# Grouped-query attention and the modulated norms of a chained transformer kernel: the values' projection moved last, the last queries' head work moved beside it and into the pair loop, rounding one step later, norms in fused pieces

## The reference, cut to what matters

```python
h = rms_norm(x, g_norm[i]) * (1.0 + sc) + sh        # twice in each layer; sc, sh differ for tokens and context

z = h @ w_qkv                                       # 1024 -> 16 query heads, 4 key heads, 4 value heads of 64
q, k = rms_norm(q, g_q), rms_norm(k, g_k)           # over the 64 features of each head
q, k = apply_rope(q, cos, sin), apply_rope(k, ...)  # only for the 256 tokens, not for the context
p = softmax(q @ k.T * 64**-0.5)                     # tokens see 512 keys, context sees 256
y = merge(p @ v) @ w_out
x = x + gate * y
```

## Time and profile before

| | us |
|---|---|
| median of 3 executions | 3028.16 (3027.71 to 3032.05) |
| the profiled execution | 3027.03 |
| its span, first to last instruction | 3025.2 |
| PE busy in the span | 2884.8 (95%) |
| DVE busy | 1829.3 (60%) |
| ACT busy | 1187.3 (39%) |
| POOL busy | 305.2 (10%) |

### The profile page before, as it was taken

The page is one execution under the profiler, slowest core; times in us unless marked ns, Lnnn a source line. Parts: engine busy times, 40 slices in busy tenths (PEclk is TensorE's granted clock), DMA queues, the critical chain, the costliest instruction groups (busy, mean ns, idle before and its releaser), DMA issues.

```text
span 3025.2 us, 43358 instructions
## 1 busy us (share of the span) xinstructions
PE 2884.8 (95%) x18438; PEld 2347.4 (78%) x18438; DVE 1829.3 (60%) x2548; ACT 1187.3 (39%) x1667; POOL 305.2 (10%) x284
## 2 busy tenths in 40 slices
PE   8999888998999999999999999998999999998999
PEld 7888888997864788877657887875678887774899
DVE  4477766555456466664875677556646775546454
ACT  3245564445234422234244222344442223425443
POOL 1000001101000201112011111200120011000110
PEclk9999999999999999999999999999999999998999
DMA  8836324454211244432113444330034443211353
GB/s 294 332 132 238 126 84 168 170 189 159 98 42 42 91 188 153 183 138 99 69 43 139 153 181 167 125 109 29 16 139 165 171 179 112 99 70 42 140 181 126
DMA packets 59617, 407.01 MB, mean 135 GB/s; under 512 B 6520, under 2 KB 9848, under 8 KB 11168
## 3 DMA queue, kind: packets, MB, share of 16 engines
q1 hardware_dynamic: 58224, 400.00, 36.1%
q0 software_dynamic: 1200, 4.23, 0.5%
HBM read 402.60 MB, written 1.09 MB: 133 GB/s over the span
## 4 chain that ended last, share of the span: by engine, by line
PE 83%; DVE 8%; ACT 5%; issue 2%; POOL 0%; DMA 0%; DVEq 0%; ACTq 0%
PE bank L600 25%; PE bank L602 24%; PE bank L601 24%; DVE wlo L1970 3%; ACT whi L1336 2%; PE bank L1089 1%; ACT part L1593 1%; PE bank L1139 1%; PE bank L1214 1%; PE bank L1083 1%; PE bank L700 1%; PE bank L1093 1%; ACT xnhi L1596 1%; PE bank L1230 1%; PE bank L724 0%
## 5 line engine op out<-in xcount | busy, mean ns | idle before, releaser
L1970 DVE TENSOR_TENSOR wlo<-raw,whi 128x2048 fp32r<-128x2048 f32 x281 | 647.3, 2304 | 457.4 <-ACT whi L1336 457.3
L1336 ACT CAST whi<-raw 128x2048 fp32r<-128x2048 f32 x281 | 535.3, 1905 | 617.8 <-PE bank L602 612.1
L600 PE MATMUL bank<-xnhi,whi 128*128 128x512 f32 (+1 forms) x1760 | 663.6, 377 | 39.2 <-DVE xnlo L2383 18.8
L602 PE MATMUL bank<-xnhi,wlo 128*128 128x512 f32 (+1 forms) x1760 | 649.6, 369 | 0.0
L601 PE MATMUL bank<-xnlo,whi 128*128 128x512 f32 (+1 forms) x1760 | 647.8, 368 | 0.0
L600 PEld LDWEIGHTS bank<-xnhi,whi 128*128 128x128 f32 x1760 | 336.0, 191 | 136.7 <-issue 59.9
L602 PEld LDWEIGHTS bank<-xnhi,wlo 128*128 128x128 f32 x1760 | 336.1, 191 | 57.0
L601 PEld LDWEIGHTS bank<-xnlo,whi 128*128 128x128 f32 x1760 | 336.6, 191 | 53.8 <-issue 0.2
L600 PE MATMUL bank<-hidhi,whi 128*128 128x512 f32 (+1 forms) x1024 | 373.3, 365 | 0.0
L601 PE MATMUL bank<-hidlo,whi 128*128 128x512 f32 (+1 forms) x1024 | 372.4, 364 | 0.0
L602 PE MATMUL bank<-hidhi,wlo 128*128 128x512 f32 (+1 forms) x1024 | 372.1, 363 | 0.0
(11 more groups left out here) (328 smaller groups left out, 4058.9 us busy)
## 6 DMA issues: line engine op xcount, KB each, us to landing
raw<-in_wall SPq DMA_DIRECT2D x317, 1024.0 KB, 4.8
vraw<-in_wall SPq DMA_DIRECT2D x60, 1024.0 KB, 4.8
x<-in_x SPq DMA_DIRECT2D x2, 1024.0 KB, 6.8
bias<-relative_offsets POOLq DMA_DIRECT2D x2, 768.0 KB, 7.2
x<-relative_offsets POOLq DMA_DIRECT2D x2, 768.0 KB, 9.7
out<-x SPq DMA_DIRECT2D x1, 1024.0 KB, 4.8
vec<-in_vec SPq DMA_DIRECT2D x1, 665.0 KB, 10.0
aqk<-aqk POOLq DMA_DIRECT2D x2, 256.0 KB, 3.3
```

The costliest lines, as they stand in the source:

```text
L600: mm(out, wh, xh, start=first, stop=False)
L602: return mm(out, wl, xh, start=False, stop=last)
L1336: nc.scalar.copy(b.whi[u % SPL][:], b.raw[pos % RAW][:]).then_inc(*R.made("hi_ready"))
L1970: ttn(b.wlo[u % SPL][:], b.raw[blocks[u] % RAW][:], b.whi[u % SPL][:], ALU.subtract).then_inc(*R.made("lo_ready"))
```

## The change

It does five things.

1. In `unit_plan` the values' block moves behind the four blocks of queries. `HEADS_OF_BLOCK` loses its empty entry, and the entries of blocks 2 to 4 are the queries.
2. Between the two chunks of the values' block PE does the last queries' head sums, the rotation of the block before, and the first scores. DVE's `take_values` does the block before's rotation, the last scaling and the first maxima between its two copies. ACT runs `head_rstd(4)` behind the block.
3. The rotation of the last block (u = 4) goes into step 0 of the pair loop on PE, into bank 3, and into step 1 on DVE.
4. ACT rounds a finished pair at n % 4 == 2 from n = 6 on, behind that step's exponentials.
5. In the norms DVE multiplies by scale and `rstd` in one instruction, and the lower half adds the shift and subtracts the upper half in one instruction; both are 256 wide, since scale and shift differ for tokens and context. ACT keeps one instruction for each half, from the part straight to `xn[0]`; its cast and its wait between are gone.

In the diff the plan comes first, then the parts of PE, of ACT and of DVE.

```diff
-            u.extend((("att_k", 0), ("att_q", 0), ("att_v", 0), ("att_q", 1), ("att_q", 2), ("att_q", 3)))
+            u.extend((("att_k", 0), ("att_q", 0), ("att_q", 1), ("att_q", 2), ("att_q", 3), ("att_v", 0)))
...
-HEADS_OF_BLOCK = ((8, 9), (0, 1), (), (2, 3), (4, 5), (6, 7))
+HEADS_OF_BLOCK = ((8, 9), (0, 1), (2, 3), (4, 5), (6, 7))
+def turned_heads(b, u, n):
+    return b.bank[6 + n][:, 0:S] if u < 4 else b.bank[VALUE_BANKS[1]][:, n * S:(n + 1) * S]
...
+        def heads_and_scores(_):
+            heads_before(5)
+            pe.wait_ge(R.sems["chunk_taken"], 2 * at["att_v"])
+            pe.wait_ge(R.sems["keys_swapped"], 32)
+            scores(0)
-        stage(1, b.xn, T2, tokens_out=True, beside=lambda k: heads_before(2))
-        stage(3, b.xn, T2, beside=lambda k: heads_before(3 + k))
-        pe.wait_ge(R.sems["chunk_taken"], 2 * at["att_out"])
-        pe.wait_ge(R.sems["keys_swapped"], 32)
-        scores(0)
-        head_sums(5)
-        rotate(4)
-        rotate(5)
+        stage(3, b.xn, T2, beside=lambda k: heads_before(2 + k))
+        stage(1, b.xn, T2, tokens_out=True, between=heads_and_scores)
         pe.wait_ge(*R.next("rot_taken", 2))
         scores(1)
...
             turn(n)
+            if n == 0:
+                pe.wait_ge(R.sems["chunk_taken"], 2 * at["att_out"])
+                rotate(4)
+            if n == 5:
+                pe.wait_ge(*R.next("rot_taken", 2))
...
-                fn(p[:, o:o + S], p[:, o:o + S], ACT.Identity, scale=b.modg[i % 2][:, sc:sc + 1],
-                   bias=b.mod[i % 2][:, sh:sh + 1]).then_inc(*R.made("act_step"))
-            act.wait_ge(*R.own("act_step"))
-            nc.scalar.copy(b.xn[0][:, c, 0:t], p[:, 0:t]).then_inc(*R.made("part_hi"))
+                last = fn(b.xn[0][:, c, o:o + S], p[:, o:o + S], ACT.Identity, bias=b.mod[i % 2][:, sh:sh + 1])
+            last.then_inc(*R.made("part_hi"))
...
-            if n >= 5 and n % 4 == 1:
+            if n >= 6 and n % 4 == 2:
                 part(b.xn[0][:, n // 4 - 1, :], width=T2)
...
-            ttn(b.xn[1][:, c, 0:t], b.part[(first + c) % 4][:, 0:t], b.xn[0][:, c, 0:t], ALU.subtract) \
-                .then_inc(*R.made("part_lo"))
+            for s, o in streams(t):
+                last = stt(b.xn[1][:, c, o:o + S], b.part[(first + c) % 4][:, o:o + S], mcol(i, 3 * which, c, s),
+                           b.xn[0][:, c, o:o + S], ALU.add, ALU.subtract)
+            last.then_inc(*R.made("part_lo"))
...
-            ttn(part(t), b.x[:, c, 0:t], b.rstd[:, 0:t], ALU.mult).then_inc(*R.made("part_ready"))
+            p = part(t)
+            for s, o in streams(t):
+                sc = 2 * (which * KC + c) + s
+                last = stt(p[:, o:o + S], b.x[:, c, o:o + S], b.modg[i % 2][:, sc:sc + 1], b.rstd[:, o:o + S],
+                           ALU.mult, ALU.mult)
+            last.then_inc(*R.made("part_ready"))
...
-        maxima(0)
-        take_rotated(4)
-        scale_heads(5)
-        take_rotated(5)
+        def take_values(_):
+            for c in range(2):
+                chunk()
+                cp(b.av[:, 2 * c:2 * c + 2, :], bank_of(c)[:].rearrange("p (a n) -> p a n", a=2)) \
+                    .then_inc(*R.made("chunk_taken"))
+                if c == 0:
+                    take_rotated(3)
+                    scale_heads(4)
+                    maxima(0)
...
             if n:
                 take_turned(n - 1)
+            if n == 1:
+                take_rotated(4)
```

More of the change, by code:

```diff
@@ L1195, in rotate @@
                 pe.wait_ge(*R.next("qn_ready"))
-                if u:
+                if 0 < u < 4:
                     pe.wait_ge(*R.next("rot_taken"))
-                mm(bank[6 + n][:, 0:S], b.rope[:, 0:P], b.aqk[:, c, 0:S], start=True, stop=True) \
-                    .then_inc(*R.made("rot_ready"))
+                last = mm(turned_heads(b, u, n), b.rope[:, 0:P], b.aqk[:, c, 0:S], start=True, stop=True)
+                if u < 4:
+                    last.then_inc(*R.made("rot_ready"))
+            if u == 4:
+                last.then_inc(*R.made("rot_ready", 2))
         def heads_before(u):
@@ L1591, in operand_parts @@
             for s in range(t // S):
[L1592 to L1596 removed]
+                o, sh = s * S, 2 * (3 * which * KC + c) + s
+                last = fn(b.xn[0][:, c, o:o + S], p[:, o:o + S], ACT.Identity, bias=b.mod[i % 2][:, sh:sh + 1])
+            last.then_inc(*R.made("part_hi"))
             g["part"] += 1
@@ L1769, in head_squares @@
                 fn(b.part[n][:], b.aqk[:, c, :], ACT.Square).then_inc(*R.made("head_squares"))
-            if not HEADS_OF_BLOCK[u]:
-                R.n["evac"] += 2
         def exponent(n):
@@ L1789, in attention @@
         stage(2, head_squares, ahead=True)
-        stage(1, lambda k: head_squares(2))
-        stage(3, lambda k: head_squares(3 + k))
-        head_rstd(5)
+        stage(3, lambda k: head_squares(2 + k))
+        stage(1)
+        head_rstd(4)
         for n in range(len(PAIR_STEPS)):
@@ L2657, in take_rotated @@
                 dve.wait_ge(*R.next("rot_ready"))
-                ttn(b.part[2][:, 0:S], bank[6 + n][:, 0:S], sin, ALU.mult).then_inc(*R.made("dve_step"))
+                ttn(b.part[2][:, 0:S], turned_heads(b, u, n), sin, ALU.mult).then_inc(*R.made("dve_step"))
                 step(ttn(b.part[2][:, S:T2], b.aqk[:, c, 0:S], cos, ALU.mult))
@@ L2666, in take_heads @@
                 cp(b.aqk[:, ch, :], bank_of(n)[:]).then_inc(*R.made("chunk_taken"))
-            if not HEADS_OF_BLOCK[u]:
-                for c in range(2):
-                    chunk()
-                    cp(b.av[:, 2 * c:2 * c + 2, :], bank_of(c)[:].rearrange("p (a n) -> p a n", a=2)) \
-                        .then_inc(*R.made("chunk_taken"))
             if u >= 2:
```

5 lines of the change are left out of this document (2 added, 3 removed).

## The result

| | before | after |
|---|---|---|
| median of four runs each, us | 3027.93 (3027.38 to 3032.05) | 3009.34 (3007.09 to 3010.44) |
| profiled execution: time, span, us | 3027.0, 3025.2 | 3007.1, 3004.9 |

The ratio is 0.9931, with a 95% interval of 0.9919 to 0.9944: 0.7% faster, where 3010 was predicted.

A forecast was written before the change was run, and what follows sets the result against it. PE was busy for 95% of the span, and a chain through three engines set the pair loop's period. 7.3 + 9.0 + 1.6 - 0.7 = 17.2 us off 3027.0 gave 3009.8, predicted as 3010, range 3005 to 3020.

The forecast's parts named there:

- The front: Gap ahead of the pair loop and rotation in steps 0 and 1: 8.9 won less 1.6, 7.3 us.
- The new wait: Ahead of step 2's transposes, PE waits 1.6 us for DVE's copy behind the moved rotations; bounds 0 and 2.5.
- The half clock: Slow rotations, scores and first transposes behind the front's idle time: 3.0 us that goes with the idle time.
- The rounding: Pair loop: rounding behind the exponentials removes six 1.5 us PE waits for ACT, 9.0 us; period 12.37 to 10.87.
- thin, but enough: Pair loop: DVE's copy ends at 2120.75, PE wants it at 2120.91, a margin of 0.16 us.
- The rival of the margin: Pair loop: PE waits for DVE's copy instead, giving back 3 us or more, 3013 to 3016; chance 0.15.
- The wide norms: Seven wide norms: 32 DVE pieces at 0.404 us make 15.1 us against 15.0 before, 0.7 us lost in all.
- The loss of 4.9 us: Seven wide norms by the skill's formula, 0.424 us a piece: 0.7 us lost each, the whole at 3014.
- The last norm: Narrow norm that PE follows chunk by chunk: 8.55 us falls to 6.9, 1.6 us won.

The follow-up runs named there:

- the order alone: Kernel before with only the blocks reordered and the last rotation moved into the first steps; attention stretch 231.47 us against 240.15, ratio 0.997.
- the filled gap: Kernel before with unread 128 x 512 matmuls put into PE's two long waits ahead of the pair loop; attention stretch 237.88 us against 240.15, ratio 1.0002.
- the product of two columns: Changed kernel plus an unread 128 x 2 VectorE product behind each of seven gated products; attention stretch 231.25 us against 222.05.
- The norms alone: Kernel before with only the changed kernel's norms (ACT's cast gone, DVE's pieces fused); ratio to before 0.9995, last stretch 193.4 us against 195.9.

## Why the prediction came out right

**The front, 7.3 us predicted, 8.65 measured** (8.68 in the run of the order alone). The idle time went as counted: 4.26 us less, where 5.9 less the new wait of 1.58 make 4.3. The new wait was predicted at 1.6, at the place and under the name that it has. That it came so close is in part luck: from the end of the values' block PE reached these transposes after 6.75 us (2068.51 to 2075.26) instead of 7.0, and DVE's copy ended after 8.28 us (2076.79) instead of 8.6; the two errors cancel. The half clock, priced at 3.0 from three rows, was 2.8 by the filled gap. What was mis-sized is the busy part: 4.39 us less in all against these 3.0. From start to start the three rows give 3.4 (1.05, 1.37 and 0.96), since the two scores behind the block take 1.49 us from start to start (2068.51 to 2070.00), less than the 1.73 of the loop's rows that the prediction took for full speed. The slow scores at 2081.80, which the count had left out, give 0.2 (0.90 us against 0.70). The values' two chunks give 0.4: 11.71 us before (2012.32 to 2024.03), 5.65 and 5.66 now. Some 0.4 us stay unassigned.

**The rounding, 9.0 predicted, 9.47 measured.** The releaser that was named is gone, the next in line (the copy) is 0.18 us ahead as counted with 0.16, and VectorE's wait for the scores shrank to 0.3 us. The period fell by 1.57 us rather than 1.50, times six. But the step that found the margin "thin, but enough" was incomplete. It counted VectorE's work up to the copy and treated POOL's product as a producer only, one that "comes later too, and is asked for only a whole pair later". It does not come later: ACT's rounding still waits for VectorE's gated product and starts 0.71 us behind that product's start, as before (2118.62 and 2119.33; 2085.37 and 2086.08), and POOL's product starts 1.41 us behind it in both kernels. Only the exponentials now run ahead of the rounding instead of behind it. And POOL's product is also a neighbour: the scaling that the copy stands behind starts 0.04 us or less ahead of it, in every period of both kernels. Both chains begin with the same gated product, one through VectorE's reductions, the other through ACT's rounding, so a VectorE that is late as a whole moves both; what decides is only what stands between the product and the scaling. The change put nothing there. Had it put 0.15 us of work there, 9.2 of the 9.5 us would have been lost and the kernel had stood near 3019, as in the run with the product of two columns. The rival of the margin had named the right releaser for this case, the copy, but not the cause, and its 3013 to 3016 were too small a price. So the forecast was right here with a luck that it had not seen.

**The wide norms, 0.7 us loss predicted, none seen.** A piece is 0.397 us from start to start rather than 0.404, and the norm of layer 0 lasts 14.88 us (1028.22 to 1043.10) against 15.02 before. That is VectorE's work as predicted, with the sign of a small difference wrong. The norms alone left the attention stretch at 240.19 against 240.15. The loss of 4.9 us that the prediction had estimated from the Trainium skill's formula ("VectorE: DVE Perf Modes", the section on the TRN2 errata) did not come, and the formula is not at fault: its 0.424 us is how long one tensor_tensor of 256 columns lasts, and the rows of the last norm before have 0.42 to 0.43. The prediction had used it as the distance between two starts, which is shorter: 0.34 us between the rows at 2830.81 and 2831.15, and 0.397 us for the pieces, which last 0.48 each.

**The last norm, 1.6 us predicted, 2.5 to 3.4 measured in the last stretch** (norms alone, and the changed kernel). VectorE's part is 6.96 us (2812.37 to 2819.33), predicted 6.9, against 8.55. The mechanism is right. What comes on top can be read from two matmuls of PE, the first on the norm's last chunk and the 27th behind it, before and after:

```profile
2837.88 0.58 PE L600 MATMUL bank<-xnhi,whi 128*128 128x256 f32 x1
...
2842.12 0.28 PE L600 MATMUL bank<-xnhi,whi 128*128 128x256 f32 x1
...
2819.53 0.38 PE L606 MATMUL bank<-xnhi,whi 128*128 128x256 f32 x1
...
2822.99 0.39 PE L606 MATMUL bank<-xnhi,whi 128*128 128x256 f32 x1
```

Counted from the norm's start, the first comes 1.44 us earlier (8.60, 7.16) and the second 2.22 (12.84, 10.62). The 0.8 us between are PE's half clock, which lasts 6.8 us in the record of before and reaches to 2840.00, past the norm: its matmuls are 0.21 us apart there and 0.12 behind it. The prediction had priced the chain alone and not the clock that hangs on it. In the changed kernel the norm's half clock costs nothing up to this point: it is 3.4 us in one profile and none in the other, and both have 10.62. What is gained behind it, up to 1.2 us, is not shown to be the change's: the last stretch lies between 191.4 and 193.7 us in the nine profiles with the new pieces, and between 195.7 and 196.3 in the four with the old.

**The sum.** 17.2 us predicted. The spans of the profiled executions differ by 20.3: 18.1 and 3.4 us, less the 1.2 of layer 3, a stretch that moves by more than that between two executions of one program. Their times differ by 19.9, the medians by 18.6. The front, the rounding and the last norm gave more than predicted and the wide norms lost nothing, some 4.3 us in all; layer 3's mixer took 1.2 of them back. That the median lies only 0.7 us from 3010 is therefore in part luck.

## What to carry to other kernels

When a stage is bound by a chain, move the piece that the chain doesn't need, and count for each move what stands behind it on every queue: the one wait that this change created was found in that way, at its place and with its releaser. A margin in a count of one engine's work is only as good as the list of its neighbours: look for GpSimd's instructions in the same few hundred nanoseconds, and see whether an operation of VectorE that reads and writes only SBUF starts before or after them. If both hang on the same instruction, as here, being late does not matter; what is put between does. To measure a margin, add a small dummy piece of work in two sizes; a cost that does not grow with the size points to an event that was missed, and not to a lack of room.

## What the runs showed of the hardware that was not expected

- A tensor_scalar of VectorE on 128 x 2 in SBUF, 0.17 us by itself, lasts until the end of a GpSimd tensor_tensor that started before it (0.60, 1.00 and 1.13 us in three kernels). Two of 128 x 1 in the same place are not held (0.21 us for both). Copies from PSUM and reductions from PSUM beside the same product kept their durations.
- TensorE's matmuls of 256 columns are not always equally far apart at full clock. At the end of the values' block they are 0.11 us apart in the changed kernel and 0.12 in the kernel before. The cause is open; no run was made for it. The first two rows are of the changed kernel:

```profile
2067.74 0.28 PE L606 MATMUL bank<-whi,xnhi 128*128 128x256 f32 x1
2067.85 0.28 PE L607 MATMUL bank<-wlo,xnhi 128*128 128x256 f32 x1
...
2023.67 0.28 PE L600 MATMUL bank<-whi,xnhi 128*128 128x256 f32 x1
2023.79 0.28 PE L601 MATMUL bank<-wlo,xnhi 128*128 128x256 f32 x1
```

- Layer 3's mixer took from 234.3 to 244.0 us in kernels that differ there in the norm's pieces at most, and 237.3 and 239.7 in two executions of one kernel, at mean clocks of 0.91 to 0.95. Differences of whole times below 5 us say little here without the stretches.
